# Forgetting attention: the first two query blocks as one unit, a new order of the last heads, and a level's copy ahead of the gate's exponential

## The reference, cut to what matters

```python
# layer 1, per head of the delta rule: solve a unit triangular system
m = jnp.where(strict, beta[..., :, None] * kk * decay, 0.0)
sol = lax.linalg.triangular_solve(m, rhs, left_side=True, lower=True, unit_diagonal=True)
# layer 1, the gate of the stick-breaking heads
o_sb = merge_heads(stick_breaking_attention(q_sb, k_sb, v_sb)) * jax.nn.silu(sb_gate)
# layer 2, forgetting heads: softmax with a log-decay sum on every key
sf = jnp.einsum('bqhd,bkhd->bhqk', qf, fk).astype(jnp.float32) * (FOX_HEAD_DIM ** -0.5)
sf = sf + jnp.transpose(cq, (0, 2, 1))[..., :, None] - cum_k[..., None, :]
pf = jax.nn.softmax(jnp.where(causal, sf, NEG), axis=-1)
of = jnp.einsum('bhqk,bkhd->bqhd', pf.astype(fv.dtype), fv)
```

## Time and profile before

| | |
|---|---|
| median of 3 runs | 1095.16 us (1094.94 to 1095.47) |
| the profiled execution | 1094.89 us, of which its span is 1093.6 us |
| instructions | 14878 |
| busy TensorE / ScalarE / VectorE / GpSimd | 1081.6 / 567.8 / 540.4 / 435.8 us |
| granted TensorE clock over the span | 0.998 |

### The profile page before, as it was taken

The page is one execution under the profiler, slowest core; times in us unless marked ns, Lnnn a source line. Parts: engine busy times, 40 slices in busy tenths (PEclk is TensorE's granted clock), DMA queues, the critical chain, the costliest instruction groups (busy, mean ns, idle before and its releaser), DMA issues.

```text
span 1093.6 us, 14878 instructions
## 1 busy us (share of the span) xinstructions
PE 1081.6 (99%) x5669; PEld 886.6 (81%) x5669; DVE 540.4 (49%) x1151; ACT 567.8 (52%) x1082; POOL 435.8 (40%) x236
## 2 busy tenths in 40 slices
PE   8999999999999999999999999999999999999998
PEld 8877878778887788888778777789888888888886
DVE  3739789788765224142445455535111115544444
ACT  6555767767777642353556566554222224333333
POOL 4334342342532444553142332345444446444441
PEclk9999999999999999999999999999999999999999
DMA  9133121221322332723222321222333334323312
GB/s 259 48 96 88 42 75 39 79 60 40 95 58 63 92 97 97 232 77 81 79 78 59 96 79 58 77 87 79 105 97 97 97 97 131 100 97 97 97 57 77
DMA packets 140530, 97.24 MB, mean 89 GB/s; under 512 B 9014, under 2 KB 125091, under 8 KB 140459
## 3 DMA queue, kind: packets, MB, share of 16 engines
q1 hardware_dynamic: 138728, 95.03, 29.6%
q10 hardware_dynamic: 1730, 1.25, 0.4%
HBM read 94.14 MB, written 2.91 MB: 89 GB/s over the span
## 4 chain that ended last, share of the span: by engine, by line
PE 90%; DVE 6%; ACT 2%; issue 1%; DMA 1%; SPq 0%; POOL 0%; ACTq 0%; DVEq 0%
PE bank L467 28%; PE bank L1189 14%; PE bank L1207 14%; PE bank L508 5%; PE bank L886 4%; PE bank L860 4%; PE bank L870 4%; PE bank L1220 2%; DVE bank L2008 1%; DVE multipliers L2006 1%; PE bank L482 1%; PE bank L682 1%; PE bank L1035 1%; PE bank L997 1%; PE bank L1017 1%
## 5 line engine op out<-in xcount | busy, mean ns | idle before, releaser
L2469 POOL TENSOR_TENSOR ring<-raw_ring,ring 128x1024 fp32r<-128x1024 f32 x160 | 388.6, 2432 | 564.8 <-ACT ring L1234 564.8
L467 PE MATMUL bank<-hT,ring 128*128 128x512 f32 x1536 | 394.7, 402 | 0.5 <-ACT rawsb L1309 0.5
L467 PEld LDWEIGHTS bank<-hT,ring 128*128 128x128 f32 x1536 | 278.0, 188 | 57.9 <-issue 6.5
L1234 ACT CAST ring<-raw_ring 128x1024 fp32r<-128x1024 f32 x160 | 167.2, 1047 | 109.6 <-PE bank L1207 88.8
L1189 PE MATMUL bank<-hT,ring 128*128 128x512 f32 x672 | 152.5, 389 | 0.0
L1207 PE MATMUL bank<-ring,ring_u 128*128 128x512 f32 x672 | 152.5, 389 | 0.0
L1207 PEld LDWEIGHTS bank<-ring,ring_u 128*128 128x128 f32 x672 | 126.2, 188 | 26.2
L1189 PEld LDWEIGHTS bank<-hT,ring 128*128 128x128 f32 x672 | 126.1, 188 | 26.1
L2444 DVE TENSOR_TENSOR ring_u<-u,ring_u 128x1024 fp32r<-128x1024 f32 x32 | 80.7, 2529 | 73.8 <-ACT ring_u L1808 73.8
L2449 DVE TENSOR_TENSOR u<-u 128x512 f32<-128x512 f32 x32 | 22.9, 714 | 138.8 <-ACT u L1815 138.8
L1815 ACT ACTIVATE u<-bank 128x512 f32<-128x512 f32 x32 | 19.1, 598 | 114.8 <-PE bank L1189 108.3
(11 more groups left out here) (293 smaller groups left out, 1488.4 us busy)
## 6 DMA issues: line engine op xcount, KB each, us to landing
raw_ring<-in_w_in SPq DMA_DIRECT2D x144, 256.0 KB, 3.3
raw_ring<-in_w_up SPq DMA_DIRECT2D x64, 256.0 KB, 3.2
raw_ring<-in_w_down SPq DMA_DIRECT2D x64, 256.0 KB, 2.8
raw_ring<-in_w_out SPq DMA_DIRECT2D x32, 256.0 KB, 2.8
x<-in_x SPq DMA_DIRECT2D x8, 512.0 KB, 5.1
raw_ring<-in_w_branch_sb SPq DMA_DIRECT2D x8, 256.0 KB, 2.9
raw_ring<-in_w_branch_gdn SPq DMA_DIRECT2D x8, 256.0 KB, 3.3
cum<-cums SPq DMA_DIRECT2D x4, 512.0 KB, 5.3
```

The source lines that it names most:

```text
L467: p = pe.matmul(bank, m.slab_k8(n % 4)[:, a, k, :], m.hT[:, b, k, :], start=term == 0, stop=term == 23)
L1234: act.copy(m.ring[:, q, 0, :], m.raw_ring[:, q, :]).then_inc(s.slab_hi[q], 1)
L2469: pool.tensor_tensor(m.ring[:, q, 1, :], m.raw_ring[:, q, :], m.ring[:, q, 0, :].bitcast(F32), ALU.subtract).then_inc(s.slab_lo[q], 1)
```

## The change

Layer 2: query blocks 0 and 1 of a forgetting head become one unit. Both are scored into one bank side by side (columns 0 to 127 and 128 to 383), one mask matmul of 256 columns serves both, and the maxima, exponentials and copies of the two stand next to each other. Blocks 2 and 3 stay units of their own, now numbered 1 and 2. The steps of the semaphores shrink from 9 and 16 to 7 and 14. In passes 0 to 2 the visit of the old second block between `diff_rows_T` and `diff_av` goes away, and the unit's transposes stand where the second block's did, one `diff_av` earlier; VectorE and ScalarE take the differential maxima and exponentials ahead of the forgetting ones, and ScalarE's `tile_b(g)` comes after the four exponentials. The order of pass 3 is set anew on all three engines. Layer 1: `stick_gate` is parted into the logarithm and the exponential, and in passes 0 to 2 level 5's copy stands between them.

```diff
+FOX_UNITS = ((0, 1), (2,), (3,))
+FOX_STEPS = (0, 6, 10, 14)
+FOX_ACT = (0, 4, 6, 8)
+
+def fox_parts(u):
+    at = 0
+    for n, t_ in enumerate(FOX_UNITS[u]):
+        yield n, t_, at, at + (t_ + 1) * P
+        at += (t_ + 1) * P
```

The transfer of the decay sums waits for the same step under its new number (`sums_for`):

```diff
-            sp.wait_ge(s.f_dve[0], 16 * (i - 2) + 13)
+            sp.wait_ge(s.f_dve[0], 14 * (i - 2) + 11)
```

The scores on TensorE:

```diff
-    def fox_z(i, t_):
+    def fox_z(i, u):
...
         for k, (a, b) in enumerate(PARTS):
-            for h in range(2):
-                hp = slice(64 * h, 64 * h + 64)
-                pe.matmul(banks[6 + h][:, 0:w], qf[hp, a, t_ * P:w], kf[hp, b, 0:w], start=k == 0, stop=k == 2)
+            for n, t_, low, high in fox_parts(u):
+                for h in range(2):
+                    hp = slice(64 * h, 64 * h + 64)
+                    pe.matmul(banks[6 + h][:, low:high], qf[hp, a, t_ * P:(t_ + 1) * P], kf[hp, b, 0:high - low],
+                              start=k == 0 and n == 0, stop=k == 2, skip_group_check=n > 0)
         for h in range(2):
-            pe.matmul(banks[6 + h][:, t_ * P:w], m.ident_b, m.causal_b, start=False, stop=True, skip_group_check=True).then_inc(s.f_ps[h], 1)
+            if u == 0:
+                o = banks[6 + h].rearrange("p (n w) -> p n w", n=2)[:, :, 0:P]
+                mask = m.causal_b.unsqueeze(1).broadcast_to([P, 2, P])
+            else:
+                t_ = FOX_UNITS[u][0]
+                o, mask = chunk(banks[6 + h], t_), m.causal_b
+            pe.matmul(o, m.ident_b, mask, start=False, stop=True, skip_group_check=True).then_inc(s.f_ps[h], 1)
```

TensorE's order in passes 0 to 2:

```diff
         fox_z(i, 0)
-        tiles.to(31)
-        fox_rows_T(i, 0, 0)
-        tiles.to(34)
-        fox_rows_T(i, 1, 0)
         tiles.to(51)
         diff_rows_T(i, 1, 0, pairs)
         tiles.to(54)
         diff_rows_T(i, 0, 0, pairs)
-        fox_z(i, 1)
         tiles.to(58)
         diff_av(i, 1, 0, pairs)
+        fox_rows_T(i, 0, 0)
+        fox_rows_T(i, 1, 0)
         tiles.to(63)
         diff_av(i, 0, 0, pairs)
-        fox_rows_T(i, 1, 1)
-        fox_rows_T(i, 0, 1)
         tiles.to(69)
         diff_z_pair(i, 1, 1, pairs)
         diff_z_pair(i, 0, 1, pairs)
-        fox_z(i, 2)
+        fox_z(i, 1)
```

TensorE's new order in pass 3, behind `diff_z(i, 1, 0, 1)`, which stands as before (added lines alone):

```diff
+    tiles.to(26)
+    fox_rows_T(i, 1, 0)
+    fox_rows_T(i, 0, 0)
+    tiles.to(29)
+    diff_rows_T(i, 0, 0, last_pairs)
+    tiles.to(33)
+    diff_rows_T(i, 1, 0, last_pairs)
+    fox_z(i, 1)
+    tiles.to(36)
+    diff_av(i, 0, 0, last_pairs)
+    tiles.to(39)
+    diff_av(i, 1, 0, last_pairs)
+    tiles.to(41)
+    diff_z(i, 0, 1, 0, last_pairs)
+    tiles.to(45)
+    diff_z(i, 0, 1, 1, last_pairs)
+    diff_z(i, 1, 1, 0, last_pairs)
+    tiles.to(48)
+    fox_rows_T(i, 0, 1)
+    fox_rows_T(i, 1, 1)
+    diff_z(i, 1, 1, 1, last_pairs)
+    tiles.to(52)
+    fox_z(i, 2)
+    tiles.to(54)
+    diff_rows_T(i, 0, 1, last_pairs)
+    tiles.to(57)
+    diff_rows_T(i, 1, 1, last_pairs)
+    diff_av(i, 0, 1, last_pairs)
+    tiles.to(61)
+    diff_av(i, 1, 1, last_pairs)
+    tiles.to(65)
+    fox_rows_T(i, 0, 2)
+    fox_rows_T(i, 1, 2)
+    tiles.to(68)
     fox_av(i)
     diff_mix(i, 5)
     tiles.to(72)
```

ScalarE in layer 1, passes 0 to 2:

```diff
         stick_exp(i, 2)
+        stick_gate_log(i)
+        delta_level(i, 5)
         stick_gate(i)
-        delta_level(i, 5)
```

ScalarE in layer 2, passes 0 to 2:

```diff
         fox_v(i)
-        fox_exp(i, 0, 0)
-        fox_exp(i, 1, 0)
-        tile_b(g)
         diff_exp(i, 1, 0, 0)
-        fox_p(i, 0, 0)
-        diff_exp(i, 0, 0, 0)
         diff_exp(i, 1, 0, 1)
+        diff_exp(i, 0, 0, 0)
         diff_exp(i, 0, 0, 1)
-        fox_p(i, 1, 0)
+        tile_b(g)
+        fox_exp(i, 0, 0)
+        fox_exp(i, 1, 0)
         diff_p(i, 0, 0, 2)
         diff_p(i, 1, 0, 4)
+        fox_p(i, 0, 0)
+        fox_p(i, 1, 0)
         tile_b(g + 1)
```

ScalarE, the end of the new order in pass 3 (added lines alone):

```diff
+    diff_p(i, 0, 1, 4)
+    fox_exp(i, 0, 2)
+    fox_exp(i, 1, 2)
+    diff_p(i, 1, 1, 5)
+    diff_square(i, 0, 1)
+    diff_square(i, 1, 1)
+    split(SLABS_OUT2 + 5)
+    fox_p(i, 0, 2)
+    fox_p(i, 1, 2)
     fox_mix(i)
     diff_mix(i, 5)
```

VectorE: `fox_max` takes both parts of a unit and negates both maxima in one instruction, `fox_recip` serves both, `fox_normed` takes one after the other. Its order at the start of passes 0 to 2 (added lines alone):

```diff
         diff_max(i, 1, 0, 0, 4)
+        diff_max(i, 1, 0, 1, 5)
+        diff_max(i, 0, 0, 0, 2)
+        diff_max(i, 0, 0, 1, 3)
         fox_max(i, 0, 0)
         fox_max(i, 1, 0)
+        diff_weights(i, 1, 0)
+        diff_weights(i, 0, 0)
         fox_recip(i, 0, 0)
```

VectorE, towards the end of the new order in pass 3 (added lines alone):

```diff
+    diff_max(i, 1, 1, 1, 5)
+    diff_weights(i, 0, 1)
+    diff_weights(i, 1, 1)
+    fox_max(i, 0, 2)
+    fox_max(i, 1, 2)
+    diff_o(i, 0, 1, 4)
+    fox_recip(i, 0, 2)
...
```

More of the change, by code:

```diff
@@ L1067, in tensor_program @@
         diff_z_pair(i, 0, 1, pairs)
-        fox_z(i, 2)
-        tiles.to(86)
-        fox_rows_T(i, 0, 2)
-        tiles.to(91)
-        fox_rows_T(i, 1, 2)
-        tiles.to(97)
-        tiles.to(102)
-        fox_z(i, 3)
+        fox_z(i, 1)
+        tiles.to(86)
+        fox_rows_T(i, 0, 1)
+        tiles.to(91)
+        fox_rows_T(i, 1, 1)
+        tiles.to(102)
+        fox_z(i, 2)
         tiles.to(109)
@@ L1687, in diff_mix, with fox_exp, fox_p @@
         act.copy(m.mix[:, 0, i, :], banks[bank]).then_inc(s.d_mhi, 1)
-    def fox_exp(i, h, t_):
-        sc = fox_rows[h][:, 0:(t_ + 1) * P]
-        st = m.stat[:, 16 + 4 * h:18 + 4 * h]
-        act.wait_ge(s.f_dve[h], 16 * i + 4 * t_ + 2)
-        act.activation(sc, sc, ACT.Exp, bias=st[:, 0:1], accum_out=st[:, 1:2]).then_inc(s.f_act[h], 1)
-    def fox_p(i, h, t_):
-        w = (t_ + 1) * P
-        act.wait_ge(s.f_ps[h], 9 * i + 2 * t_ + 2)
-        dst = m.fox_wT[:, 3 - t_, 4 - t_:5, :] if h else m.fox_wT[:, t_, 0:t_ + 1, :]
-        act.copy(dst.rearrange("p c f -> p (c f)"), banks[6 + h][:, 0:w]).then_inc(s.f_act[h], 1)
+    def fox_exp(i, h, u):
+        st = m.stat[:, 32 + 6 * h:38 + 6 * h]
+        act.wait_ge(s.f_dve[h], 14 * i + FOX_STEPS[u] + len(FOX_UNITS[u]) + 1)
+        for n, _, low, high in fox_parts(u):
+            sc = fox_rows[h][:, low:high]
+            act.activation(sc, sc, ACT.Exp, bias=st[:, n:n + 1], accum_out=st[:, 2 + n:3 + n]).then_inc(s.f_act[h], 1)
+    def fox_p(i, h, u):
+        act.wait_ge(s.f_ps[h], 7 * i + 2 * u + 2)
+        for _, t_, low, high in fox_parts(u):
+            dst = m.fox_wT[:, 3 - t_, 4 - t_:5, :] if h else m.fox_wT[:, t_, 0:t_ + 1, :]
+            act.copy(dst.rearrange("p c f -> p (c f)"), banks[6 + h][:, low:high]).then_inc(s.f_act[h], 1)
     def fox_mix(i):
-        act.wait_ge(s.f_ps[0], 9 * (i + 1))
-        act.wait_ge(s.f_ps[1], 9 * (i + 1))
+        act.wait_ge(s.f_ps[0], 7 * (i + 1))
+        act.wait_ge(s.f_ps[1], 7 * (i + 1))
         act.copy(m.mix[:, 0, 4 + i, :], banks[6]).then_inc(s.f_mhi, 1)
@@ L1758, in scalar_program @@
     fox_exp(i, 1, 0)
[L1759 removed]
     diff_exp(i, 0, 0, 1)
+    diff_exp(i, 1, 0, 1)
+    split(SLABS_OUT2 + 2)
     fox_p(i, 1, 0)
     fox_p(i, 0, 0)
[L1763 to L1774 removed]
+    diff_p(i, 0, 0, 4)
+    split(SLABS_OUT2 + 3)
+    diff_p(i, 1, 0, 5)
+    fox_exp(i, 0, 1)
+    fox_exp(i, 1, 1)
+    diff_square(i, 0, 0)
+    diff_square(i, 1, 0)
+    diff_exp(i, 0, 1, 0)
+    diff_exp(i, 0, 1, 1)
+    diff_exp(i, 1, 1, 0)
+    fox_p(i, 0, 1)
+    fox_p(i, 1, 1)
+    diff_exp(i, 1, 1, 1)
+    split(SLABS_OUT2 + 4)
+    diff_p(i, 0, 1, 4)
     fox_exp(i, 0, 2)
     fox_exp(i, 1, 2)
[L1777 to L1779 removed]
+    diff_p(i, 1, 1, 5)
+    diff_square(i, 0, 1)
+    diff_square(i, 1, 1)
+    split(SLABS_OUT2 + 5)
     fox_p(i, 0, 2)
     fox_p(i, 1, 2)
[L1782 to L1791 removed]
     fox_mix(i)
@@ new lines, in fox_recip, with fox_normed @@
+    def fox_recip(i, h, u):
+        st, count = stat[:, 32 + 6 * h:38 + 6 * h], len(FOX_UNITS[u])
+        dve.wait_ge(s.f_act[h], 8 * i + FOX_ACT[u] + count)
+        dve.reciprocal(st[:, 4:4 + count], st[:, 2:2 + count]).then_inc(s.f_dve[h], 1)
+    def fox_normed(i, h, u):
+        st, count = stat[:, 32 + 6 * h:38 + 6 * h], len(FOX_UNITS[u])
+        dve.wait_ge(s.f_dve[h], 14 * i + FOX_STEPS[u] + count + 2)
+        for n, _, low, high in fox_parts(u):
+            sc = fox_rows[h][:, low:high]
+            dve.tensor_scalar(sc, sc, st[:, 4 + n:5 + n], None, ALU.mult).then_inc(s.f_dve[h], 1)
```

199 lines of the change are left out of this document (54 added, 145 removed).

## The result

The changed kernel takes 1097.82 us (median of 11 runs, 1097.49 to 1098.40) against 1095.16 of the kernel before (11 runs beside it). The ratio is 1.0024, with a 95% interval of 1.0016 to 1.0032: slower by 2.7 us, where 1094.9 was forecast. Its span is 1096.2 us, 2.6 longer. TensorE's granted clock is 0.999 over the span, for 0.998 before, so both run at the 2.4 GHz level. All times and ratios in this document are of runs with a granted clock of 0.996 or more; one of the 11 runs of experiment 6, at 0.654, took 1531.15 us and is left out.

A forecast was written before the change was run, and what follows sets the result against it. TensorE, busy 99% of the span, was taken as the bound, so only less issue or less waiting pays. Terms -0.35 - 0.2 + 0.35 = -0.2 gave 1094.9 us against the median; 80% range 1093.0 to 1096.4.

The forecast's parts named there:

- Part B: Layer 2, passes 0 to 2: merged unit saves 0.40 a pass, a new copy wait returns 0.33; -0.2 us in all.
- Part A: Layer 1, first three passes: level's copy ahead of the gate's exponential; -0.35 us, bounds 0 and -1.95.
- 0.12 is all that TensorE can be early: Layer 1, first state product: VectorE's copy of the state's first chunk limits the gain to 0.12 us a pass.
- Rival 3: Layer 2, passes 0 to 2: merged unit costs what its two visits did; sum +1.0, 1096.2 us; chance 10%.
- Rival 4: Layer 2, three passes: late ScalarE cast makes TensorE wait for GpSimd's weight slab; 1097.9 us; chance 6%.
- Part C: Layer 2, fourth pass: new order on three engines; +0.35 us, bounds -1.0 and +1.5.
- I carried the new order forward with the same durations: Layer 2, fourth pass: method of timing the new order, each instruction keeping its earlier length; gave +0.35 us.
- the 0.7 and 0.7 foreseen: Fourth pass: TensorE waits 0.7 for ScalarE's last differential copy; wants last mixed rows at 707.4, which come at 708.1.
- a slab cast of 1.05 ahead of the last two forgetting copies: Fourth pass, ScalarE: this cast precedes copies ending at 703.6; product with the values starts at 703.7, against 702.90.
- +1.5, if each of three waits is 0.4 longer: Upper bound for the fourth pass of layer 2, whose expected change was +0.35 us.
- Part C at either bound alone stays within 0.2%: Claim that the fourth pass alone cannot make a measurable change; 0.2% is about 2.2 us.
- The forecast's own list of what would prove it wrong: Signs: passes shortening by more than 0.3 each, or any wait over 0.5 repeating in each.

The follow-up runs named there:

- experiment 6: Changed kernel with root before slab 5's subtraction, slab 2's cast later, copies swapped, last differential copy before an exponential, slab 5 cast right behind slab 4: 1092.97 us.
- experiment 4: Changed kernel, but in passes 0 to 2 ScalarE copies half 1's transposed weights ahead of half 0's, in the order TensorE uses them: 1096.54 us.
- experiment 7: Kernel before, with only layer 1's level copy placed between the gate's logarithm and exponential in passes 0 to 2: 1094.55 us, ratio 0.9995.
- experiment 2: Changed kernel, but in pass 3 ScalarE casts output slab 2 after its two copies of forgetting weights instead of before: 1095.75 us.
- experiment 1: Changed kernel, but GpSimd takes the last head's inverse root of the mean square ahead of slab 5's subtraction: 1096.58 us.

## Why the prediction was wrong

**What bounds the kernel** held: TensorE issues less by what Part B said (without its wait, in experiment 4, the stretch is 1.36 shorter than before, where the bound for no wait was 1.2), and everything else was a matter of waits.

**Part A** was right in that VectorE clips the gain, and a little small in size: -0.49 here and -0.51 in experiment 7, for -0.35. The term mis-sized is "0.12 is all that TensorE can be early": a pass period, from one solve to the next, is 188.64 - 117.87 = 70.77 after, for 177.46 - 106.50 = 70.96 between the old waits. That gives 0.19 a pass. The limit was also put in the wrong place. It lies at the solve (waits of 0.6 in all), where the forecast saw only "a little more room". At the first state product TensorE waits for nothing: VectorE's copy for it (line 2052) ends at 122.71, and TensorE takes it at 123.17. The trace has a reason on VectorE: its line 1905 (1897 before) beside GpSimd's subtraction took 1.32 us from 117.73, and 1.89 from 117.95 before, since that subtraction now ends at 118.50 and not at 119.29. That VectorE's order was "not touched" did not mean that its durations stayed. That this is the whole of the difference was not tested.

**Part B** was right: -0.08 for -0.2, with the wait at the product measured as 0.29 plus 0.12 of slow start (experiment 4) where 0.28 and 0.05 were forecast. The pairs of 128 and 256 columns and the masks cost 0.93 for 0.88. Rival 3 (the unit costs what the two visits did) falls: 0.93 against 0.47 + 0.64 = 1.11. Rival 4 did not occur, though the cast came as late as forecast: it stands at 535.66, as ScalarE's timeline of the changed kernel has it, and as the whole pass runs 0.76 earlier there (532.34 for 533.10), that is the forecast's 536.4. No wait of TensorE for GpSimd follows:

```profile
535.66 1.04 ACT L1245 CAST ring<-raw_ring 128x1024 fp32r<-128x1024 f32 x1
```

Luck has a part in this. The moved cast brought the subtraction beside the scaling of 536.75 in all three passes, so VectorE's weights came 2.1 us later than the 540.2 of the forecast (541.55, or 542.3 on its time scale), which left 0.11 to spare in pass 0. The step that failed in Part C was wrong here too, and only its cost was hidden.

What the forecast did not draw from its own rows is that this wait is a matter of the order of two copies, and could be had back (experiment 4).

**Part C** is the step that failed, twice. The first failure is the sentence "I carried the new order forward with the same durations". Apart from the two new waits, TensorE's pieces came about where the forecast put them: of the later waits, 0.48 and 0.47 answer to the 0.7 and 0.7 foreseen, and 0.33 to one for the last forgetting copies, to which it gave no length of its own. But VectorE's duration depends on what GpSimd does in that moment, and the cast of slab 2, which the change moved ahead of two copies, brings the subtraction to 681.77, against 683.91 before. The first round's weighting (line 2311) was carried over at 0.75 us, and took 2.94. That was worth 2.07 us (experiment 2). The trace of before already had such a case: line 1897 at 117.95 took 1.89, where it takes 0.69 otherwise, with GpSimd's subtraction at 116.90 to 119.29:

```profile
116.90 2.39 POOL L2469 TENSOR_TENSOR ring<-raw_ring,ring 128x1024 fp32r<-128x1024 f32 x1 [12.53 <-ACT ring L1234]
```

After the trace, the Trainium skill: the page SBUF — State Buffer, section "Who interferes with whom", says that the port pair which VectorE and GpSimd share is an exclusive lock; a VectorE instruction with two SBUF inputs, or in a mode that uses both ports, and a GpSimd instruction that reads SBUF exclude each other for a whole instruction, and the second to start is fully blocked. The 2.94, the 1.65 and the 3.21 agree with it, but for the order of the records (below). The same section lists scaling by a scalar among the instructions that can enter such a mode, and the 2.21 with one input agrees. Had the forecast weighed it, it would have looked for GpSimd's subtractions beside lines 2311 and 2320.

The second failure is one of omission. The prediction followed ScalarE's cast of slab 5 as "a slab cast of 1.05 ahead of the last two forgetting copies" and did not go on to its reader. On GpSimd that slab's subtraction stands ahead of the root in a fixed order, and the change moved the cast from far ahead of the root's inputs (690.17) to behind them (702.10). So the root, which runs at 702.85 when it goes first (experiment 1), ran at 705.66. That was worth 1.24 us.

The bound "+1.5, if each of three waits is 0.4 longer" was therefore too small: it took in that known waits grow, and not that a wait arises in a place that had none. Part C measured +3.41, and with the bound falls "Part C at either bound alone stays within 0.2%", on which the chance of slower rested. (Two sums are also a little off: by the lower bound of Part C, -1.0, the terms give 1093.6 and not 1093.9, and 708.1 against 707.8 gives +0.3 and not +0.35. Neither matters here.) Of the rivals, rival 4 had the nearest thought (a slab, a cast and GpSimd), but in the wrong passes and by the wrong path: TensorE never waited for a slab. The harm came from a subtraction that ran earlier, beside VectorE (slab 2's), and from one that ran later, ahead of the root (slab 5's).

The forecast's own list of what would prove it wrong names longer passes and repeated waits, and neither occurred. It had no line for two single waits in pass 3.

## What to carry to other kernels

When a change moves an instruction on one engine, follow what it releases on the next one, and then what stands beside and behind that: here two casts on ScalarE, for which nothing waited directly, set the starts of two GpSimd instructions, of which one held VectorE and one delayed the root, 3.3 us in all. In this kernel GpSimd's subtractions are best seen as blocks of 2.4 us in which VectorE should not begin an instruction with two inputs in SBUF or a wide scaling from SBUF, and placed where VectorE reads banks or idles. If two copies feed two products, give them the order of the products.
